# Three edits in a two-block model kernel: one root a token and head in the scans' normalisation, a first projection that begins with half its weights, sorted keys for dilated attention

## What is computed

```
DILATED_PATTERNS = ((128, 1), (512, 4), (2048, 16))     # window, dilation; 8 heads of 64

def dilated_attention(q, k, v, window, dilation):
    blk = window // dilation                            # always 128
    def to_blocks(t):                                   # every dilation-th token to one sequence
        t = t.reshape(B, H, L, dilation, Dh).transpose(0, 1, 3, 2, 4)
        return t.reshape(B, H, dilation, n_blk, blk, Dh)
    qb, kc, vc = to_blocks(q), with_prev(to_blocks(k)), with_prev(to_blocks(v))
    scores = jnp.einsum('bhrnqd,bhrnkd->bhrnqk', qb, kc)
    ...

def rms_norm_2(x, g):
    y = xf * lax.rsqrt(jnp.mean(xf * xf, axis=-1, keepdims=True) + EPS)
    return (y * g.astype(jnp.float32)).astype(x.dtype)

def hgrn_branch(...):                                   # o_l: 4 heads of 64 channels a token
    out_l = from_heads(rms_norm_2(o_l, gain))
    ...
y = jnp.concatenate([y_conv, att * g_att, out_l * silu(hz), y_four], axis=-1) @ w_out
```

## Time and profile before

| | us |
|---|---|
| median of 3 runs | 5314.19 |
| lowest and highest | 5302.58, 5317.26 |
| the profiled execution's own time | 5306.81 |
| its span in the profile | 5304.8 |
| TensorE busy | 4750.0 (90%) |
| VectorE busy | 2483.5 (47%) |
| ScalarE busy | 1688.8 (32%) |
| GpSimd busy | 1208.3 (23%) |

### The profile page before, as it was taken

How to read it: one execution, slowest core, us unless ns; L and a number is a source line. 1 busy time by engine, 2 the same in 40 slices (tenths; PEclk the granted TensorE clock), 3 DMA queues, 4 the chain that set the end, 5 groups by cost and what they waited for, 6 DMA issues and landing times. The chain is left out here.

```text
span 5304.8 us, 66741 instructions
## 1 busy us (share of the span) xinstructions
PE 4750.0 (90%) x26209; PEld 3269.9 (62%) x26209; DVE 2483.5 (47%) x4843; ACT 1688.8 (32%) x3122; POOL 1208.3 (23%) x1239
## 2 busy tenths in 40 slices
PE   6989998997969988899999898989896999988989
PEld 3447776775758655745554576876665644544767
DVE  3322345556643656635541264444566445501544
ACT  3332225553353111223441233242112234321431
POOL 1000020003410101418880001001122267830000
PEclk8989999998979999899999999999998999999999
DMA  5012104334420000100001202200000100002022
GB/s 190 8 56 72 40 1 158 133 104 162 149 99 17 1 9 1 57 17 11 11 9 38 72 16 92 88 28 17 9 1 31 36 9 13 7 25 86 16 72 95
DMA packets 149818, 272.41 MB, mean 51 GB/s; under 512 B 11645, under 2 KB 82693, under 8 KB 147845
## 3 DMA queue, kind: packets, MB, share of 16 engines
q1 hardware_dynamic: 145188, 257.67, 14.3%
q10 hardware_dynamic: 4320, 10.49, 0.5%
HBM read 198.92 MB, written 69.19 MB: 51 GB/s over the span
## 5 line engine op out<-in xcount | busy, mean ns | idle before, releaser
L1489 PE MATMUL ps_proj<-features_high,weights_high 128*128 128x512 f32 (+1 forms) x880 | 347.2, 394 | 60.6 <-DVE features_low L1552 31.2
L1489 PE MATMUL ps_proj<-features_high,weights_low 128*128 128x512 f32 (+1 forms) x880 | 341.1, 388 | 0.0
L1489 PE MATMUL ps_proj<-features_low,weights_high 128*128 128x512 f32 (+1 forms) x880 | 340.2, 387 | 0.0
L1703 PE MATMUL ps_s<-qf,kb 64*128 64x128 f32 x3264 | 235.7, 285 | 60.9 <-DVE scores_t L1873 55.5
L2436 ACT ACTIVATE weight_ring<-ps_st 128x1024 f32<-128x1024 f32 x193 | 197.9, 1025 | 249.1 <-PE ps_st L2323 243.2
L1703 PEld LDWEIGHTS ps_s<-qf,kb 64*128 64x128 f32 x3264 | 200.8, 188 | 112.6 <-issue 59.8
L1552 DVE TENSOR_TENSOR features_low<-h_t,features_high 128x1024 fp32r<-128x1024 f32 (+1 forms) x140 | 159.8, 1144 | 186.7 <-ACT features_high L1517 186.4
L2941 PE MATMUL ps_o<-w_out_high,y_high 128*128 128x512 f32 x544 | 217.4, 400 | 27.4 <-DVE y_low L2959 19.9
L1489 PEld LDWEIGHTS ps_proj<-features_high,weights_high 128*128 128x128 f32 x880 | 171.6, 195 | 110.0 <-DVE weights_low L1543 31.3
L2484 DVE TENSOR_REDUCE features_or_outputs<-ps_max 128x2 f32<-128x1024 f32 x128 | 156.7, 1224 | 166.0 <-PE ps_max L2293 166.0
L728 PE MATMUL ps_proj<-weights_high,features_high 128*128 128x512 f32 x512 | 207.0, 404 | 27.8 <-DVE features_low L823 27.8
(11 more groups left out here) (428 smaller groups left out, 10542.7 us busy)
## 6 DMA issues: line engine op xcount, KB each, us to landing
weight_ring<-in_w_in_dram SPq DMA_DIRECT2D x40, 1024.0 KB, 5.6
weight_ring<-in_w_mod_dram SPq DMA_DIRECT2D x48, 512.0 KB, 4.1
t_rows<-t_rows SPq DMA_DIRECT2D x64, 256.0 KB, 2.3
x_res<-h_rows SPq DMA_DIRECT2D x32, 512.0 KB, 3.5
res<-result SPq DMA_DIRECT2D x48, 264.0 KB, 2.1
res_rows<-res SPq DMA_DIRECT2D x48, 264.0 KB, 3.8
h_t<-v_rows SPq DMA_DIRECT2D x3, 4096.0 KB, 13.9
q_rows<-q_rows SPq DMA_DIRECT2D x34, 256.0 KB, 2.6
```

The source lines that it names most:

```text
L1489: mm = pe.matmul(bank[:, 0:n], w_[:, k0 + k, i * P:(i + 1) * P], f_[:, k, 0:n], start=start, stop=stop)
L1703: mm = pe.matmul(pS[pr][h][:, i * P:(i + 1) * P], kb[lo, s % 2, pr, i * P:(i + 1) * P], q, start=True, stop=True)
```

## The change

**Projection.** ScalarE and VectorE now make the first half of the first job's weights, the features of step 0, the second half of the weights, and the features of step 1.

**Dilated attention.** GpSimd gets two sets of four copies of 128x2048, one for each pair of heads. The first set, at the stage's start, writes the keys into `yaT` sorted by their remainder by 4, so that every fourth key stands side by side. The second, when the last scores with dilation 1 are done, writes them back into `KTt` sorted by their remainder by 16. The scores with dilation 4 read their keys from `yaT`, those with dilation 16 from `KTt`, without a step. The queries are read as before. TensorE waits for `keys_sorted` before the first scores of each of the two patterns. The four loads into `yaT` move to units 69, 73, 77 and 81 and wait for the sorted keys too.

**Normalisation.** The squares are now the stationary operand (four 128x128 pieces for 512 tokens), and two columns of the matrix of means stream past: the means come out with tokens on the partitions, 2 columns for 128 tokens. One root and one reciprocal of 128x36 (128x32 in layer 1) serve a whole group of channels. ScalarE then repeats each value 64 times along the row (`o_repeat`), and TensorE multiplies with the identity to bring it back to channels on partitions (`ps_on`). VectorE multiplies straight from PSUM. Two banks hold means, four hold the spread values.

```diff
@@ stage_qkvg, ScalarE; VectorE has the same order with low() @@
-            weights(0)
-            for s in range(NB):
-                high(s)
+            weights(0, (0,))
+            high(0)
+            weights(0, (1,))
+            high(1)
@@ stage_dilated @@
+    KS = (KTt, yaT, KTt)
...
-                if u % 8 == 1 and 1 <= u // 8 <= CT:
-                    c = u // 8 - 1
+                c = u // 4 - NT - 1
+                if u % 4 == 1 and 0 <= c < CT:
+                    sp.wait_ge(kp.h, kp.at(8))
                     sp.dma_start(yaT[:, c, :], ya_d[:, c, :]).then_inc(yld.h, 16)
...
+                if p >= 1 and u % (2 * NT) == 0:
+                    pe.wait_ge(kp.h, kp.at(4 * p))
+                k1 = (k0 % dil) * (S // dil) + k0 // dil
...
-                                       KTt[lo:lo + HD, pair, k0:k0 + dil * (w * P - 1) + 1:dil], start=True, stop=True)
+                                       KS[p][lo:lo + HD, pair, k1:k1 + w * P], start=True, stop=True)
...
+        @block.gpsimd
+        def _(pool):
+            for pr in range(4):
+                pool.tensor_copy(yaT[:, pr, :].rearrange("p (r i) -> p r i", r=4),
+                                 KTt[:, pr, :].rearrange("p (i r) -> p r i", r=4)).then_inc(kp.h, 1)
+            pool.wait_ge(smm.h, smm.at(2 * NT))
+            pool.wait_ge(kp.h, kp.at(4))
+            for pr in range(4):
+                pool.tensor_copy(KTt[:, pr, :].rearrange("p (a r i) -> p r a i", a=4, r=4),
+                                 yaT[:, pr, :].rearrange("p (r i a) -> p r a i", r=4, a=4)).then_inc(kp.h, 1)
@@ stage_hgrn_norm @@
+            for u in range(NC + 1):
+                square(u)
+            root(0)
+            for u in range(NC):
+                if NC + 1 + u < NU:
+                    square(NC + 1 + u)
+                repeat(u)
+            root(1)
+            for u in range(NC, NU):
+                repeat(u)
...
-                pe.matmul(ps[u % 2][:, 0:n], env.headmean[:, :], o2[:, u % 2, 0:n], start=True, stop=True).then_inc(mm_.h, 1)
+                for j in range(n // P):
+                    t = c0 // P + j
+                    mm = pe.matmul(pm[pr][:, 2 * t:2 * t + 2], o2[:, u % 2, j * P:(j + 1) * P], heads, start=True, stop=True)
...
+                for j in range(n // P):
+                    mm = pe.matmul(ps[u % 4][:, j * P:(j + 1) * P],
+                                   re[:, u % 2, j, :, :].rearrange("p h c -> p (h c)"), env.ident[:, :],
+                                   start=True, stop=True)
...
-                dve.reciprocal(rr[:, u % 2, 0:n], rr[:, u % 2, 0:n]).then_inc(rc.h, 1)
+                if u % NC == 0:
+                    dve.reciprocal(rr[:, pr, :, :], rr[:, pr, :, :]).then_inc(rc.h, 1)
-                                         in1=rr[:, u % 2, 0:n], op0=ALU.mult, op1=ALU.mult).then_inc(sd.h, 1)
+                                         in1=ps[u % 4][:, 0:n], op0=ALU.mult, op1=ALU.mult).then_inc(sd.h, 1)
```

More of the change, by code:

```diff
@@ L746, in weights @@
                     act.wait_ge(stp.h, stp.at((2 * j - 3) * JS))
-                for half in range(2):
+                for half in halves:
                     ks = slice(half * KT // 2, (half + 1) * KT // 2)
@@ L802, in _, with weights @@
         def _(dve):
-            def weights(j):
-                for half in range(2):
+            def weights(j, halves=(0, 1)):
+                for half in halves:
                     ks = slice(half * KT // 2, (half + 1) * KT // 2)
@@ L812, in weights @@
                            .then_inc(wls.h, 1)
+                if 1 not in halves:
+                    return
                 for g in range(2):
@@ L843, in rope @@
                 ins.then_inc(rd.h, 1)
-            weights(0)
-            for s in range(NB):
-                low(s)
+            weights(0, (0,))
+            low(0)
+            weights(0, (1,))
+            low(1)
             for s in range(NS):
@@ L1933, in stage_hgrn_norm @@
     units = [(pr, c) for pr in range(2) for c in chunks]
-    sq, mm_, rt, rc, sd, yo = (env.sem(n) for n in ("o_squared", "o_mean", "o_root", "o_recip", "o_scaled", "o_gated"))
+    NU, NC = len(units), len(chunks)
+    TN = sum(n for _, n in chunks) // P
+    sq, mm_, rt, rc, ex, bc, sd, yo = (env.sem(n) for n in ("o_squared", "o_mean", "o_root", "o_recip", "o_repeated", "o_spread",
+                                                           "o_scaled", "o_gated"))
     with ExitStack() as ctx:
@@ L1958, in _, with means @@
         @block.tensor
         def _(pe):
[L1960 removed]
+            def means(u):
+                pr, (c0, n) = units[u]
                 pe.wait_ge(sq.h, sq.at(u + 1))
[L1962 to L1964 removed]
+                for j in range(n // P):
+                    t = c0 // P + j
+                    mm = pe.matmul(pm[pr][:, 2 * t:2 * t + 2], o2[:, u % 2, j * P:(j + 1) * P], heads, start=True, stop=True)
+                mm.then_inc(mm_.h, 1)
@@ new lines, in spread @@
+            def spread(u):
+                pr, (c0, n) = units[u]
+                pe.wait_ge(ex.h, ex.at(u + 1))
+                if u >= 4:
+                    pe.wait_ge(sd.h, sd.at(u - 3))
+                for j in range(n // P):
+                    mm = pe.matmul(ps[u % 4][:, j * P:(j + 1) * P],
+                                   re[:, u % 2, j, :, :].rearrange("p h c -> p (h c)"), env.ident[:, :],
+                                   start=True, stop=True)
+                mm.then_inc(bc.h, 1)
@@ L1966, in _ @@
+            for u in range(NC + 2):
+                means(u)
+            for u in range(NC):
+                if u + NC + 2 < NU:
+                    means(u + NC + 2)
+                spread(u)
+            for u in range(NC, NU):
+                spread(u)
         @block.vector
@@ L1981, in _ @@
                 pool.tensor_tensor(o, o, zT[:, pr, c0:c0 + n], ALU.mult).then_inc(yo.h, 1)
-    for s_ in (sq, mm_, rt, rc, sd, yo):
-        s_.base += len(units)
+    for s_, c_ in ((sq, NU), (mm_, NU), (rt, 2), (rc, 2), (ex, NU), (bc, NU), (sd, NU), (yo, NU)):
+        s_.base += c_
 def stage_qkv2(env, layer, hT, q_d, room, spare, KA, KB, VN, qtiles):
```

51 lines of the change are left out of this document (28 added, 23 removed).

## The result

| | before | after |
|---|---|---|
| median, us (12 executions each) | 5309.88 | 5287.61 |
| lowest and highest | 5302.42, 5317.26 | 5263.35, 5299.61 |
| the profiled execution's own time | 5306.81 | 5263.35 |

The ratio is 0.995 (0.9939 to 0.9961): the change gains 22 us of the 55 that were forecast, and the median lies 6 us above the range. The profiled execution of after is its fastest of twelve, 24 us under its median, so a comparison of the two profiles flatters the change. There are therefore a second and a third trace of the same kernel (e4, e12) and a second one of before (e8).

The account below looks back on a forecast made before the run. TensorE bounds dilated attention, VectorE the normalisations. Gains of 37.0 (keys without a step), 2.3 (projection) and 18.9 (normalisation) less 3 (sorting) make 55.2 us off 5306.8, so 5251.6; forecast 5254 us, range 5230 to 5282.

Parts of the forecast that it names:

- One-block groups: Dilated attention, score groups with one block of keys: 1.23 (dilation 4) and 1.15 us (16) to 0.75, saving 3.8 and 12.8.
- So I take 0.2: Dilated attention: the queries' remaining step was priced at 0.2 us a group, from a possible 0 to 0.3.
- the remainder of 0.34: Dilated attention: 0.34 us of a stepped group left after taking the streamed part away, read as the stationary queries' possible cost.
- rival (a): The queries' step is free (14 us more) or normalisations hold the full clock (9 more): 5240, 5245, both 5231; chance 0.15.
- Two-block groups: Dilated attention, dilation 4, groups with two blocks of keys: 2.12 to 1.27 us each, 24 groups saving 20.4 us.
- Moved and remaining loads, costed at nothing: Dilated attention: the moved loads into `yaT` still leave modulation loads in time; if not, about 1 us for each of four.
- Sorting, 3 us (0 to 9): Dilated attention: GpSimd's copies, 4.5 us each, are hidden but hold VectorE's L1088 in the second set, costing 3 us.
- Projection, 2.3 us: Projection's start: two weight instructions fewer ahead let VectorE's features, and so TensorE, begin earlier; gain 2.3 us (2 to 2.4).
- Normalisation, 18.9 us: Both normalisations: blocks of 31 and 28.5 us instead of 41.1 and 37.3, gaining 18.9 us (−4 to +28).
- (e): Dilated attention: GpSimd's copies hold VectorE for their whole length in both sets; 5275 at 4.5 us a copy; chance 0.05.
- Rival (c): Dilated attention: a step of 4 is free and only 16 costs, losing 24.2 us of the gain: 5278; chance 0.02.
- The base: Whole kernel: gains were taken from the profiled execution's 5306.8 us, giving 5251.6; from the median of 5314.2, 5259.0.

Follow-up runs that it names:

- e4: The changed kernel run again unedited, for a second trace: median 5283.36 us, ratio 0.9957 to the kernel before.
- e12: The changed kernel run again unedited, for a third trace: median 5282.7 us over 6 executions.
- e8: The kernel before run again unedited, for a second trace: 5312.02 us.
- e7: The changed kernel with the 4 MB load of the third pattern's values cut in four, four units apart: median 5280.04 us, ratio 0.9939 to before.
- e6: The changed kernel without GpSimd's sorting copies and the waits on them, so scores read other keys: 5265.73 us, one execution.
- e13: e7 with GpSimd's whole sorting copies started one by one, each just after a small SBUF copy of VectorE's: median 5273.93 us, ratio 0.994 to before.
- e2: The kernel before with dilated attention's sorted keys and moved loads alone: median 5293.99 us, ratio 0.9971.
- e11: e7 with each of GpSimd's sorting copies also cut in four of 512 columns: median 5275.93 us, ratio 0.9941 to before.
- e1: The kernel before with the projection's new order alone: median 5311.76 us, ratio 1.0003 (0.9994 to 1.0011).

## Why the prediction was wrong

**One-block groups: the step that failed.** "So I take 0.2", for all groups. It was right for two blocks (0.17) and wrong for one (0.49 with dilation 4, 0.42 with 16); and a one-block group without any step takes 0.64, not 0.55. The sum 8 × 0.48 + 32 × 0.40 = 16.6 us became 8 × 0.10 + 32 × 0.08 = 3.4. A shared price for loads that may hide and loads that can't was the wrong model. Putting the remainder of 0.34 whole on the one-block groups would not have mended it: 0.55 + 0.34 = 0.89, and they take 1.13. At one block the keys' streaming was hidden behind the loads, so its price must not be taken off there at all. (The sum has a slip as well: with nothing kept it is 50 and not 51, so rival (a) adds 13 and not 14.)

**Two-block groups**: 0.88 instead of 0.85, right. The stage's account is 24.5 for all groups, less 5.0 for the late weights and 1.5 for the copies: 18.0, and the traces show 17.4.

**Moved and remaining loads, costed at nothing**: the four moved loads are indeed free. What I didn't look at was the one that stayed, the 4 MB load at unit 35. With TensorE faster, the weights behind it come 1.95 us late, and the clock falls: 5.0 us by e7 (where the clock doesn't fall, as in e6, only the wait). The prediction named this cover ("if that cover fails, about 1 us") for the wrong transfer.

**Sorting, 3 us (0 to 9)**: the copies take 3.9 us and not 4.5, L1110 is stretched twice, TensorE loses 1.3 us at units 30 and 32, and by e13 against e7 the whole is 1.5 us. Right in mechanism and size, as long as the clock doesn't fall; in e2 it fell. The Trainium skill, "SBUF — State Buffer", section "Who interferes with whom", gave that mechanism, and the rows 168 ns to 3.54 us agree. VectorE's copies from PSUM beside it (0.41 us) were not held, which also agrees. e11's 4.34 us, through four of GpSimd's instructions, goes beyond the one instruction that the section names. I had put the start at no cost; there L1113, a copy of 128x512 between two tiles in SBUF, lasts 4.07 us (before 0.43), until GpSimd's first copy ends. That is covered by the wait for the first modulation weights, which falls from 8.4 us to 4.5 (e6, above, gains nothing there).

**Projection, 2.3 us**: 2.51 at the first matmul, 2.5 to 3.4 in the stage, whose own scatter is about 1 us. Right, but e1 shows nothing of it in the median.

**Normalisation, 18.9 us**: blocks of 31 to 33 and 28.6 to 29.9 against 31 and 28.5, 16 to 19 us. Right, the clock as foreseen: 0.50 under the means and the first spreadings, 0.95 and more in the second group.

**The rivals.** None came. Of (e), copies that hold VectorE, 1.5 us are left, which is the forecast's own term and not the rival's 27. Rival (c)'s rule, that a step of 4 fp32 is free, is refuted for TensorE's streamed operand: the two-block groups of dilation 4 lost 0.88 us each when the step went.

**The base.** The sum went from one profiled execution and assumed that untouched stages keep their time. They moved by up to 20 us between the five traces of the table (30 with e7's), and by about 13 against the change in the mean; why against it stays open. Touched stages 17.4 + 2.6 + 17.5 = 37.5, less 13, is the gain of 24.5. The range counted the spread of three executions of one kernel (5302.6 to 5317.3) and nothing for that. So two things of like size, 13 us in the one-block groups and 13 in the untouched stages, and the 5 us of the late weights make up the difference from 55 to 24.5.

## What to carry to other kernels

A step in the streamed operand and one in the stationary one don't add to one price: take each shape's own bound, loads or streaming, and remove the one that sets the pace (here the queries' step would be worth another 17 us in the stage, 21 by its groups alone). When TensorE gets faster, list every large transfer that stays where it is, and put GpSimd's SBUF copies between VectorE's own; cut small, back to back, they held VectorE longer in the one trace here. A gain of under 1% is to be read from the touched stages and from many executions, since a microsecond's wait can cost ten at half the clock and the untouched stages shift by more than the gain.

## What was not expected of the hardware

- A stationary operand of 64x128 float32 read with a step of 4 or 16 holds a one-block group at 1.13 and 1.07 us; without it 0.64 and 0.65. One load takes 303 ns with a step of 16 and 186 without. A step of 16 costs no more than one of 4.
- VectorE's SBUF copy can wait through several GpSimd instructions: 4.34 us once, across four copies of 512 columns of about 1.06 us each (16.94/16). The other such copy of the same trace got its turn after 1.12 us.
- The same wait of TensorE (1.1 us) was followed by no slow unit in after and by 24 us at 1.2 GHz in e2.
- The time of an untouched stage goes with the place of its start between the clock's possible changes: 494.6 to 506.2 us for one attention layer, in 16 traces with one or two exceptions.
